# One-pass layer norm after a convolution: sums taken about the mean of the first 256 channels

## What is computed

```python
def layernorm(x, g, b):
    xf = x.astype(jnp.float32)
    mu = jnp.mean(xf, axis=-1, keepdims=True)
    var = jnp.mean(jnp.square(xf - mu), axis=-1, keepdims=True)
    y = (xf - mu) * lax.rsqrt(var + EPS_2)
    return (y * g.astype(jnp.float32) + b.astype(jnp.float32)).astype(x.dtype)

def conformer_conv(h, w_pw1, b_pw1, w_dw, b_dw, ln_g, ln_b, w_pw2, b_pw2):
    u = h @ w_pw1 + b_pw1
    a, gate = jnp.split(u, 2, axis=-1)
    u = a * jax.nn.sigmoid(gate)
    u = causal_dwconv_2(u, w_dw, b_dw)          # 31 taps per channel
    u = jax.nn.silu(layernorm(u, ln_g, ln_b))
    return u @ w_pw2 + b_pw2
```

## Time and profile before

| | us |
|---|---|
| three runs | 1154.23, 1154.87, 1156.58; median 1154.87 |
| the profiled execution | 1152.1, of which span 1150.3 |
| PE busy | 1083.0 (94% of the span) |
| DVE busy | 781.6 (68%) |
| ACT busy | 535.7 (47%) |
| POOL busy | 123.1 (11%) |
| mean granted TensorE clock | 0.981 of full speed |

### The profile page before, as it was taken

One profiled execution on the slowest core, in us unless ns is written; L12 is line 12 of the kernel. 1 busy time (PEld: TensorE's weight loads), 2 busy tenths in 40 slices (PEclk: granted clock), 3 DMA queues, 4 the chain that ended last, 5 costly groups with the idle time before them and its releaser, 6 DMA issues.

```text
span 1150.3 us, 22943 instructions
## 1 busy us (share of the span) xinstructions
PE 1083.0 (94%) x8721; PEld 1027.4 (89%) x8721; DVE 781.6 (68%) x1314; ACT 535.7 (47%) x917; POOL 123.1 (11%) x140
## 2 busy tenths in 40 slices
PE   5999899899999989997999999997999999999998
PEld 4989569799999979776999999996888989999998
DVE  5866467575555558884777767759866657777676
ACT  6444265454444436126644444455435555444442
POOL 0050010011111140112000010040010000000100
PEclk9999799899999999998999999999999999999999
DMA  8563115255556653320555655653630025655551
GB/s 318 164 175 101 55 37 148 91 165 184 182 182 182 183 146 115 107 75 13 171 187 183 195 183 174 193 165 110 201 115 15 2 61 165 201 180 195 177 184 65
DMA packets 46437, 165.25 MB, mean 144 GB/s; under 512 B 5152, under 2 KB 6176, under 8 KB 46240
## 3 DMA queue, kind: packets, MB, share of 16 engines
q1 hardware_dynamic: 45216, 163.24, 45.1%
q10 hardware_dynamic: 1152, 1.05, 0.4%
HBM read 162.17 MB, written 1.05 MB: 142 GB/s over the span
## 4 chain that ended last, share of the span: by engine, by line
PE 80%; DVE 14%; ACT 4%; issue 2%; DMA 0%; POOL 0%; SPq 0%; DVEq 0%; ACTq 0%
PE acc L876 15%; PE acc L878 15%; PE acc L877 15%; PE big L876 6%; PE big L878 6%; PE big L877 6%; DVE WL L1493 4%; PE mis L884 2%; DVE CD L1857 2%; PE acc L480 2%; PE big L451 1%; PE acc L937 1%; PE acc L939 1%; PE acc L938 1%; ACT WH L1244 1%
## 5 line engine op out<-in xcount | busy, mean ns | idle before, releaser
L1493 DVE TENSOR_TENSOR WL<-WR,WH 128x1024 fp32r<-128x1024 f32 x302 | 370.6, 1238 | 151.1 <-ACT WH L1244 142.7
L876 PE MATMUL acc<-XH,WH 128*128 128x256 f32 x1392 | 402.6, 289 | 21.7 <-DVE WL L1493 12.3
L878 PE MATMUL acc<-XH,WL 128*128 128x256 f32 x1392 | 394.3, 283 | 0.0
L877 PE MATMUL acc<-XL,WH 128*128 128x256 f32 x1392 | 394.0, 283 | 0.0
L1244 ACT ACTIVATE WH<-WR 128x1024 fp32r<-128x1024 f32 x302 | 313.6, 1052 | 131.7 <-PE acc L878 91.2
L876 PEld LDWEIGHTS acc<-XH,WH 128*128 128x128 f32 x1392 | 266.9, 192 | 25.8 <-issue 16.4
L877 PEld LDWEIGHTS acc<-XL,WH 128*128 128x128 f32 x1392 | 266.6, 192 | 0.9
L878 PEld LDWEIGHTS acc<-XH,WL 128*128 128x128 f32 x1392 | 266.6, 192 | 0.0
L876 PE MATMUL big<-UH,WH 128*128 128x256 f32 x608 | 170.5, 280 | 0.3 <-POOL UL L1971 0.3
L878 PE MATMUL big<-UH,WL 128*128 128x256 f32 x608 | 169.6, 279 | 0.0
L877 PE MATMUL big<-UL,WH 128*128 128x256 f32 x608 | 169.6, 279 | 0.0
(11 more groups left out here) (296 smaller groups left out, 1312.1 us busy)
## 6 DMA issues: line engine op xcount, KB each, us to landing
WR<-weights SPq DMA_DIRECT2D x302, 512.0 KB, 3.6
X<-x_t SPq DMA_DIRECT2D x4, 256.0 KB, 6.3
MEM<-mem_t SPq DMA_DIRECT2D x1, 1024.0 KB, 10.1
result_t<-X SPq DMA_DIRECT2D x4, 256.0 KB, 2.2
CON<-constants SPq DMA_DIRECT2D x1, 896.0 KB, 12.4
CBUF<-KCV ACTq DMA_DIRECT2D x4, 128.0 KB, 5.2
CBUF<-KCV ACTq DMA_DIRECT2D x4, 127.5 KB, 5.7
SML<-small_weights SPq DMA_DIRECT2D x1, 480.0 KB, 14.3
```

What stands on the lines that cost most here:

```text
L876: pe.matmul(out, wh, hi, start=start, stop=False, skip_group_check=True)
L877: pe.matmul(out, wh, lo, start=False, stop=False, skip_group_check=True)
L878: return pe.matmul(out, wl, hi, start=False, stop=stop, skip_group_check=True)
L1493: dve.tensor_tensor(WL[:, cs % SPL], WR[:, cs % RAW], WH[:, cs % SPL].bitcast(F32), ALU.subtract).then_inc(w_low, 1)
```

## The change

The layer norm's variance is computed in one pass. The mean s of the first two channel tiles (256 channels) is taken as a shift, all sums are taken of x - s, and the variance is the mean of (x - s)^2 less the square of the mean of x - s. Part by part:

- PE, pair 1: two matmuls with ones sum `CX` 0 and 1 ahead of the identity taps. DVE turns this into -s (`MU[:, 0]`) after its own taps of pair 1, and adds it to `CX` 0 and 1. For pairs 1, 2 and 3 PE adds -s into PSUM by four further identity matmuls. Pair 1 waits for `shift_done`.
- ACT: `conv_out` squares straight from PSUM right after each copy (for pairs 1 and 2); `CX` 0 and 1 are squared from SBUF once they are shifted. For pair 3 ACT squares and DVE copies, each working on the tile that the other is not reading.
- PE: the feature sums and square sums of tiles 0 to 3 stand after taps(2), those of tiles 4 and 5 between the tap matmuls of pair 3 and its last identity taps, those of tiles 6 and 7 at the end.
- DVE: mean, its square, and the variance (line 1931 of the new kernel, read from PSUM); three tiles are centred before the reciprocal deviation arrives, the others between the products; the low parts `YL` are made here and no longer on POOL.
- ACT: Ln takes the variance from `MU[:, 2]`.

```diff
+                if p == 1:
+                    for j in range(2):
+                        pe.wait_ge(sem("cx_whole"), j + 1)
+                        ins = pe.matmul(mis[:, 1, T:2 * T], ONES[:, :], CX[:, j], start=j == 0, stop=j == 1,
+                                        skip_group_check=True)
+                    ins.then_inc(sem("shift_ps"), 1)
+                if p == 3:
+                    for j in (4, 5):
+                        sum_features(j)
+                        sum_square("ln", j)
                 pe.wait_ge(sem("part_done"), 4 * p + 4)
-                for a in range(2):
+                if p == 1:
+                    pe.wait_ge(sem("shift_done"), 1)
+                for a in range(2 if p == 0 else 3):
                     for r, c, rs, cs in halves:
-                        ins = pe.matmul(big[cs, 2 * (p % 2) + r, 0:T], con("ident2")[rs], CD[rs, p % 2, c, a],
-                                        start=False, stop=a == 1, skip_group_check=True)
+                        x = CD[rs, p % 2, c, a] if a < 2 else MU[rs, 0]
+                        ins = pe.matmul(big[cs, 2 * (p % 2) + r, 0:T], con("ident2")[rs], x, start=False,
+                                        stop=a == (1 if p == 0 else 2), skip_group_check=True)
...
-                if p >= 1:
-                    sum_features(2 * p - 2)
-                    sum_features(2 * p - 1)
+                if p == 2:
+                    for j in range(4):
+                        sum_features(j)
+                        sum_square("ln", j)
             sum_features(KD - 2)
             sum_features(KD - 1).then_inc(sem("mean_ps"), 1)
-            sum_squares("ln")
+            for n, k in ((7, KD - 1), (8, KD - 2)):
+                pe.wait_ge(sq_ready, SQ_BASE["ln"] + n)
+                ins = pe.matmul(mis[:, 0, 0:T], ONES[:, :], SQ[:, k], start=False, stop=n == 8, skip_group_check=True)
+            ins.then_inc(nps_ready, 1)
...
-                for r in range(2):
-                    act.activation(CX[:, 2 * p + r], big[:, 2 * (p % 2) + r, 0:T], ACT.Copy).then_inc(sem("cx_whole"), 1)
+                for r in range(2) if p < 3 else (1, 0):
+                    if p < 3:
+                        act.activation(CX[:, 2 * p + r], big[:, 2 * (p % 2) + r, 0:T], ACT.Copy).then_inc(sem("cx_whole"), 1)
+                    elif r == 0:
+                        act.wait_ge(sem("cx_last"), 1)
+                    if p > 0:
+                        act.activation(SQ[:, 2 * p + r], big[:, 2 * (p % 2) + r, 0:T], ACT.Square).then_inc(sq_ready, 1)
...
+            act.preload_act_table_set("natural_log_exp_and_others")
             conv_out(3)
-            act.preload_act_table_set("natural_log_exp_and_others")
-            for k in range(KD):
-                act.wait_ge(sem("cx_centred"), k + 1)
-                act.activation(SQ[:, k], CX[:, k], ACT.Square).then_inc(sq_ready, 1)
-            rstd("ln", RS2)
+            act.wait_ge(sem("var_done"), 1)
+            link(act.activation(LNV[:, :], MU[:, 2], ACT.Ln, bias=EPS[:, 1:2]))
+            act.activation(RS2[:, :], LNV[:, :], ACT.Exp, scale=-0.5).then_inc(rstd_ready, 1)
...
+                if p == 2:
+                    dve.wait_ge(sem("shift_ps"), 1)
+                    dve.tensor_scalar(MU[:, 0], mis[:, 1, T:2 * T], -1.0 / (2 * P), None,
+                                      ALU.mult).then_inc(sem("shift_done"), 1)
+                    dve.wait_ge(sem("shift_done"), 1)
+                    for j in range(2):
+                        dve.tensor_tensor(CX[:, j], CX[:, j], MU[:, 0], ALU.add).then_inc(sem("cx_shifted"), 1)
+            dve.wait_ge(sem("taps_ps"), 4)
+            for r in range(2):
+                if r == 1:
+                    dve.wait_ge(sq_ready, SQ_BASE["ln"] + 7)
+                dve.tensor_copy(CX[:, 6 + r], big[:, 2 + r, 0:T]).then_inc(sem("cx_last"), 1)
             dve.wait_ge(sem("mean_ps"), 1)
-            link(dve.tensor_scalar(MU[:, :], mis[:, 1, 0:T], 1.0 / D, None, ALU.mult))
-            for k in range(KD):
-                dve.tensor_tensor(CX[:, k], CX[:, k], MU[:, :], ALU.subtract).then_inc(sem("cx_centred"), 1)
+            link(dve.tensor_scalar(MU[:, 1], mis[:, 1, 0:T], 1.0 / D, None, ALU.mult))
+            link(dve.tensor_tensor(MU[:, 0], MU[:, 1], MU[:, 1], ALU.mult))
+            dve.wait_ge(nps_ready, NORM["ln"] + 1)
+            dve.scalar_tensor_tensor(MU[:, 2], mis[:, 0, 0:T], 1.0 / D, MU[:, 0], ALU.mult,
+                                     ALU.subtract).then_inc(sem("var_done"), 1)
+            left = [centred(k) for k in range(3)]
             rstd_done("ln")
             for k in range(KD):
+                dve.wait_ge(dve_chain, left[k])
                 dve.tensor_tensor(GY[:, k], CX[:, k], RS2[:, :], ALU.mult).then_inc(gy_ready, 1)
+                if k + 3 < KD:
+                    left.append(centred(k + 3))
+                if k >= 2:
+                    y_low(k - 2)
+            y_low(KD - 2)
+            y_low(KD - 1)
```

More of the change, by code:

```diff
@@ L165, in program @@
         B = group([("SG", [P, 2, T], F32), ("AT", [P, 2, T], F32), ("UP", [P, KD, T + CONV_W - 1], F32),
-                   ("CX", [P, KD, T], F32), ("CD", [P, 2, 2, 2, T], F32), ("MU", [P, T], F32),
+                   ("CX", [P, KD, T], F32), ("CD", [P, 2, 2, 2, T], F32), ("MU", [P, 3, T], F32),
                    ("DG", [P, 2, PE_TAPS, 2, 64], F32)])
@@ L1177, in taps @@
                                   start=i == 0, stop=False, skip_group_check=True)
+                if p == 1:
[8 more added lines that the diff above has]
+                        sum_square("ln", j)
                 pe.wait_ge(sem("part_done"), 4 * p + 4)
-                for a in range(2):
+                if p == 1:
+                    pe.wait_ge(sem("shift_done"), 1)
+                for a in range(2 if p == 0 else 3):
                     for r, c, rs, cs in halves:
-                        ins = pe.matmul(big[cs, 2 * (p % 2) + r, 0:T], con("ident2")[rs], CD[rs, p % 2, c, a],
-                                        start=False, stop=a == 1, skip_group_check=True)
+                        x = CD[rs, p % 2, c, a] if a < 2 else MU[rs, 0]
+                        ins = pe.matmul(big[cs, 2 * (p % 2) + r, 0:T], con("ident2")[rs], x, start=False,
+                                        stop=a == (1 if p == 0 else 2), skip_group_check=True)
                 ins.then_inc(sem("taps_ps"), 1)
             def sum_features(j):
-                pe.wait_ge(sem("cx_whole"), j + 1)
+                if j < 2:
+                    pe.wait_ge(sem("cx_shifted"), j + 1)
+                elif j < 6:
+                    pe.wait_ge(sem("cx_whole"), j + 1)
+                else:
+                    pe.wait_ge(sem("cx_last"), j - 5)
                 return pe.matmul(mis[:, 1, 0:T], ONES[:, :], CX[:, j], start=j == 0, stop=j == KD - 1,
@@ L1424, in _ @@
                 sp.to(C0 + 2 * j + 2 + AHEAD)
+                if j == 5:
+                    for r in range(2):
+                        act.wait_ge(sem("cx_shifted"), r + 1)
+                        act.activation(SQ[:, r], CX[:, r], ACT.Square).then_inc(sq_ready, 1)
                 if j % 2 == 1 and j >= 3:
                     conv_out((j - 3) // 2)
+            act.preload_act_table_set("natural_log_exp_and_others")
             conv_out(3)
-            act.preload_act_table_set("natural_log_exp_and_others")
-            for k in range(KD):
-                act.wait_ge(sem("cx_centred"), k + 1)
-                act.activation(SQ[:, k], CX[:, k], ACT.Square).then_inc(sq_ready, 1)
-            rstd("ln", RS2)
+            act.wait_ge(sem("var_done"), 1)
+            link(act.activation(LNV[:, :], MU[:, 2], ACT.Ln, bias=EPS[:, 1:2]))
+            act.activation(RS2[:, :], LNV[:, :], ACT.Exp, scale=-0.5).then_inc(rstd_ready, 1)
             for k in range(KD):
@@ L1881, in _, with centred, y_low @@
                     taps(p - 1, 9, 2 * own)
-            dve.wait_ge(sem("mean_ps"), 1)
-            link(dve.tensor_scalar(MU[:, :], mis[:, 1, 0:T], 1.0 / D, None, ALU.mult))
-            for k in range(KD):
-                dve.tensor_tensor(CX[:, k], CX[:, k], MU[:, :], ALU.subtract).then_inc(sem("cx_centred"), 1)
+                if p == 2:
[6 more added lines that the diff above has]
+            dve.wait_ge(sem("taps_ps"), 4)
+            for r in range(2):
+                if r == 1:
+                    dve.wait_ge(sq_ready, SQ_BASE["ln"] + 7)
+                dve.tensor_copy(CX[:, 6 + r], big[:, 2 + r, 0:T]).then_inc(sem("cx_last"), 1)
+            dve.wait_ge(sem("mean_ps"), 1)
+            link(dve.tensor_scalar(MU[:, 1], mis[:, 1, 0:T], 1.0 / D, None, ALU.mult))
[3 more added lines that the diff above has]
+                                     ALU.subtract).then_inc(sem("var_done"), 1)
+            def centred(k):
+                if k < 6:
+                    dve.wait_ge(sem("cx_whole"), k + 1)
+                return ch.add(dve.tensor_tensor(CX[:, k], CX[:, k], MU[:, 1], ALU.subtract))
```

(9 more changed lines are left out.)

## The result

The changed kernel takes 1160.11 us in the median of six runs (1159.82 to 1161.17), the kernel before 1154.90: a ratio of 1.0046, with a 95% interval of 1.0035 to 1.0057. That is 5.2 us slower; 1156.4 had been forecast, 1159.3 as the upper end. In a later comparison on one chip, with 10 runs against 31, the same kernel came out at 1.0026 (1.0006 to 1.0047).

What follows compares the result with a forecast made beforehand. PE was taken as the bound (busy 94%, 80% of the chain), with no cover before the last identity taps. Chain to Ln +1.7, low part -0.45, loop +0.3 gave +1.5 on 1154.87: 1156.4 us, range 1153.9 to 1159.3.

Steps and rivals of the forecast that it cites:

- The twelve sums and the added identities: Pairs 2 and 3 on PE: no cover; sums 0.47 us each, four more identity matmuls 0.45 per pair.
- The tail to Ln: From the last identity taps to Ln: 7.04 us becomes 2.9, a saving of 4.1.
- Pair 1: End of pair 1: shift sums (1.06 us) fit PE's idle 1.14; net +0.1, between -0.1 and +0.6.
- The sign of the net: Whole kernel: slower by 1.5 us, within the 0.2% (2.3 us) band of no change.
- The bounds given for the terms: Pair 1 -0.1 to +0.6, twelve sums -0.5 to +0.7, loop -0.65 to +0.2, clock 0 to +2 us.
- From there on the program is the same.: After tile 0 of pw2, whose end moves by +1.5 us: no further change counted.
- The sum: Whole kernel: +1.7 us for the chain to Ln, -0.45 low part, +0.3 loop, giving +1.5.
- ACT's squares and the earlier table load lie beside this: Pair 2: they run beside PE's sums and taps, DVE long finished, so PE alone sets the time.
- Tile 0 of pw2: First tile of pw2: first product +1.25 us, end of the tile +1.5.
- The loop of DVE and ACT: Tile 0 of pw2: DVE's order ties product k+1 to low part k-2; 0.65 us late at k = 7.
- Rival A: Tile 0 of pw2: low clock outlasts it and slows tile 1; about 1158.5 us, chance 0.31.
- the return to full speed: Tile 0 of pw2: after about 5.9 us of PE work, at 541.8, just as the tile ends.

Runs made afterwards that it cites:

- the kernel before with six sums: Six further fp32 sums that feed nothing, ahead of the last identity taps, added to the kernel before; median 1159.94 us, ratio 1.0048.
- The kernel with all sums last: The changed kernel with all sixteen feature and square sums behind the last identity taps; median 1160.12 us, ratio 1.0034 to the kernel before.

## Why the prediction was wrong

What held. The twelve sums and the added identities had no cover: +3.01 and +2.03 us for pairs 2 and 3 against 3.25 and 2.0 forecast (0.43 for a sum in place of 0.47). The tail to Ln shrank by 4.0 (7.04 to 3.04), against 4.1. Pair 1 was +0.09 against +0.1: the shift sums fitted into PE's idle time. The sign of the net was right. The bounds given for the terms add up to 1155.1 to 1159.8, not to the stated 1153.9 to 1159.3; the measured 1160.1 lies above both.

What failed, in the order of size.

1. "From there on the program is the same." It is, but it does not run in the same time. The sum took the shift of 1.5 us as a shift of the end. Both profiles of the changed kernel fall to half speed near 850 us, which costs 2.9 us each time, and neither of the kernel before does; 11 of 16 executions have a mean clock of 0.978 or less, against 15 of 89. This is about 2 of the 3.7 us by which the forecast missed, the sum having no term for it. That it does not take the changed kernel's code is shown by the kernel before with six sums; why some kernels with a delay of about 3 us have it and others do not is open.
2. Pair 2, "ACT's squares and the earlier table load lie beside this", and nothing for POOL. The identity taps and the shift delayed POOL's diagonals to 495.03, and DVE's weight split at 498.37 took 1.95 in place of 1.22. In the kernel before POOL had just finished when that split began (491.01 + 4.21 = 495.22). DVE was the releaser of PE there, so +0.6. The row of 1.95 us stood in the trace of the kernel before, at 472.46, beside POOL's diagonals of that pair, and I did not ask what had made it long. Rows of the kernel before:

```profile
469.13 4.20 POOL L1997 TENSOR_TENSOR DG<-CON,VEC 128x1152 f32<-128x1152 f32 x2 [41.30 <-PE big L1181]
472.46 1.95 DVE L1493 TENSOR_TENSOR WL<-WR,WH 128x1024 fp32r<-128x1024 f32 x1
491.01 4.21 POOL L1997 TENSOR_TENSOR DG<-CON,VEC 128x1152 f32<-128x1152 f32 x2 [17.67 <-PE big L1181]
495.21 1.22 DVE L1493 TENSOR_TENSOR WL<-WR,WH 128x1024 fp32r<-128x1024 f32 x1
```

3. Tile 0 of pw2, +0.25 forecast behind the first product, +0.8 measured. The loop of DVE and ACT was sized right (last Silu +0.69, forecast 0.65). The end was not: with the last input late, the last k step and its drain ran at half speed, 1.4 us from the last low part to the residual (545.25 to 546.65), where before it was about 0.95 (POOL's row ended at 539.96, the residual began at 540.91). The kernel with all sums last shows the same end at full speed: 0.67 less. Rival A named the low clock here; it did outlast tile 0, but cost only 0.3 in tile 1. The prediction took the return to full speed as 5.9 us behind PE's restart; here it came 7.5 us behind it (539.58 to 547.1).

The windows of the changed kernel over tile 0, which answer to the earlier trace rows:

```profile
535.00:539.00 4.00, 0.00 (x0) 0.00 (x0) 3.37 (x10) 3.64 (x7) 0.00 (x0) 0.74 0.00 0
539.00:543.00 4.00, 3.42 (x12) 2.85 (x12) 3.75 (x11) 3.77 (x9) 0.00 (x0) 0.50 0.00 0
543.00:547.00 4.00, 4.00 (x17) 3.46 (x16) 2.05 (x6) 2.68 (x6) 0.00 (x0) 0.50 0.00 0
547.00:551.00 4.00, 4.00 (x35) 4.00 (x34) 2.27 (x5) 2.45 (x5) 0.00 (x0) 0.98 0.10 18
```

The clock fell near 537 and was back at 547. The Trainium skill (TensorE: Matmul & The Clock Gate, Part 1: The HAM clock gate) has the monitor run free of the kernel. The runs agree as to the steps ahead of the stretch, which come and go between executions of the same code. That the share of executions with a low mean clock goes from 0 of 9 to 10 of 10 between kernels whose code near 850 us is the same is more than that page says.

## What to carry to other kernels

Work moved out of a serial tail is a gain only up to the idle time of the engine that it is moved onto, read at the place where it is put: here 0.25 and 0.54 us of idle were to take in 5 us of sums. When an edit delays one engine's work, look at what it then runs beside; a long duration of a common instruction in the old trace marks such a collision. And compare a stretch from a marker to a marker in the profiles before believing a median of a few microseconds: a delay in one place can change at which clock another place runs, and gains of 1.5 us vanish in that.

## What was not expected of the hardware

- A DVE operation on two SBUF inputs was held up until the two-input POOL operation beside it had ended: 2.34 us in place of 0.42 or 0.47, 1.95 in place of 1.22. The reverse was seen too: POOL's first low part took 2.28 in place of 0.73 beside DVE. Reads of PSUM by DVE (SG from `acc`, 0.42 at 498.03) were not lengthened beside the same POOL row.
- The mean granted clock of single executions sorts them into groups. Before: median 1154.0 us at 0.981 and more (61 of 89), 1158.9 at 0.978 and less (15). So where half speed falls is worth more than the whole change that was forecast.
- Sums that feed nothing, put into a 4.8 us idle stretch, kept the full clock only until the sparse work behind them; it fell at 542, where PE had not been idle for more than 0.97 us at a time. Near 850 it fell behind idle times of 1.0, 0.3 and 1.0 us.
